# First adaptation of the second block on VectorE inside the first feed-forward, and output weight parts 0 and 1 split whole among the small products

## What is computed

```python
# first block, two layers
h = rms_norm(x, ln1_gain[l]); proj = h @ w_in[l]          # 1024 -> 2866
x = x + concat(nsa(proj), mla(proj), retention(proj)) @ w_out[l]
h = rms_norm(x, ln2_gain[l])
x = x + square(relu(h @ w_up[l])) @ w_down[l]              # 1024 -> 4096 -> 1024

# second block, layers ab and cd, on tokens x and context xc
shift, scale, gate = split(silu(c) @ w_ada + b_ada, 3)     # the adaptation: 1024 -> 3072
cshift, cscale, cgate = split(silu(c_ctx) @ w_ada + b_ada, 3)
h = rms_norm_2(x, norm_g) * (1 + scale) + shift            # hc likewise from xc
```

## Time and profile before

| | us |
|---|---|
| runs | 1077.96, 1077.51, 1077.50 |
| median | 1077.51 |
| span of the profiled execution | 1076.1 |
| its own time | not listed apart; the median lies 1.4 above the span |
| TensorE busy | 1051.7 (98%) |
| VectorE busy | 751.0 (70%) |
| ScalarE busy | 549.1 (51%) |

### The profile page before, as it was taken

The page is one execution under the profiler, slowest core; times in us unless marked ns, Lnnn a source line. Parts: engine busy times, 40 slices in busy tenths (PEclk is TensorE's granted clock), DMA queues, the critical chain, the costliest instruction groups (busy, mean ns, idle before and its releaser), DMA issues. The chain is left out here.

```text
span 1076.1 us, 17324 instructions
## 1 busy us (share of the span) xinstructions
PE 1051.7 (98%) x6788; PEld 900.5 (84%) x6788; DVE 751.0 (70%) x1442; ACT 549.1 (51%) x993; POOL 63.4 (6%) x80
## 2 busy tenths in 40 slices
PE   8999999999999999999999999999999999999996
PEld 7877889899988886888998899888886687989865
DVE  5766757655556576777788888789898945824765
ACT  5543845544445454764444544452657833623563
POOL 1000000000000000001000000020051301000000
PEclk9999999999999999999999999999999999999998
DMA  9758056565564657325856566593326233943200
GB/s 344 263 197 344 3 157 195 162 201 191 192 196 163 196 196 266 120 84 185 185 196 196 160 199 197 189 305 133 110 93 260 78 118 107 257 140 118 60 21 40
DMA packets 55477, 183.33 MB, mean 170 GB/s; under 512 B 21092, under 2 KB 33764, under 8 KB 35940
## 3 DMA queue, kind: packets, MB, share of 16 engines
q1 hardware_dynamic: 55396, 182.22, 51.8%
HBM read 179.31 MB, written 2.90 MB: 169 GB/s over the span
## 5 line engine op out<-in xcount | busy, mean ns | idle before, releaser
L257 DVE TENSOR_TENSOR w_lo<-ring,w_hi 128x1024 fp32r<-128x1024 f32 x259 | 316.2, 1223 | 179.8 <-ACT w_hi L242 176.2
L242 ACT CAST w_hi<-ring 128x1024 fp32r<-128x1024 f32 x259 | 270.9, 1054 | 318.0 <-PE banks L313 317.5
L313 PE MATMUL banks<-f_hi,w_hi 128*128 128x256 f32 x512 | 144.0, 281 | 0.0
L313 PE MATMUL banks<-f_hi,w_lo 128*128 128x256 f32 x512 | 143.8, 281 | 0.0
L313 PE MATMUL banks<-f_lo,w_hi 128*128 128x256 f32 x512 | 143.8, 281 | 0.0
L313 PE MATMUL banks<-w_hi,u_hi 128*128 128x512 f32 x256 | 100.1, 391 | 0.0
L313 PE MATMUL banks<-w_hi,u_lo 128*128 128x512 f32 x256 | 99.9, 390 | 0.0
L313 PE MATMUL banks<-w_lo,u_hi 128*128 128x512 f32 x256 | 99.9, 390 | 0.0
L313 PEld LDWEIGHTS banks<-f_hi,w_hi 128*128 128x128 f32 x512 | 96.4, 188 | 0.7 <-DVE f_lo L444 0.2
L313 PEld LDWEIGHTS banks<-f_lo,w_hi 128*128 128x128 f32 x512 | 96.5, 188 | 0.5
L313 PEld LDWEIGHTS banks<-f_hi,w_lo 128*128 128x128 f32 x512 | 96.5, 188 | 0.0
(11 more groups left out here) (421 smaller groups left out, 2167.9 us busy)
## 6 DMA issues: line engine op xcount, KB each, us to landing
ring<-in_w_up SPq DMA_DIRECT2D x32, 1024.0 KB, 5.2
ring<-in_w_down SPq DMA_DIRECT2D x32, 1024.0 KB, 5.1
ring<-in_w_in SPq DMA_DIRECT2D x23, 1024.0 KB, 5.2
ring<-in_ab_ada SPq DMA_DIRECT2D x12, 1024.0 KB, 5.9
ring<-in_cd_ada SPq DMA_DIRECT2D x12, 1024.0 KB, 5.2
ring<-in_cd_in SPq DMA_DIRECT2D x12, 1024.0 KB, 5.6
ring<-in_w_out SPq DMA_DIRECT2D x8, 1024.0 KB, 7.5
ring<-in_ab_in SPq DMA_DIRECT2D x16, 512.0 KB, 4.8
```

The costliest lines, as they stand in the source:

```text
L242: nc.scalar.copy(w_hi[:, n % PARTS, :], part_source(key, q)).then_inc(hi_ready, 1)
L257: nc.vector.tensor_tensor(w_lo[:, n % PARTS, :], part_source(key, q), w_hi[:, n % PARTS, :].bitcast(F32), ALU.subtract).then_inc(part_read ...
L313: mm = nc.tensor.matmul(dst, a, b, start=first_one and i == 0, stop=last_one and i == 2, skip_group_check=shares_bank)
```

## The change

- The adaptation leaves the mixers of both layers: the products, the copies, the turning, the bias additions, their signals and their places in the ring are gone. The attention loses the split in pieces.
- In the mixers ScalarE casts output part 0 behind its tanh and part 1 behind the first turned heads; VectorE makes the two low parts behind the retention's centred values, ahead of the activation of the hidden products. The first output half is handed back to the ring after the compressed values.
- In the first feed-forward the twelve halves of ab_ada stand in the ring, each behind the feed-forward half named by ADA_BEHIND (1, 3, 5, 8, 10, 13, 15, 17, 20, 22, 25, 27). VectorE multiplies eight row blocks of 128 x 512 for each slab and condition by a factor per partition and sums them in `ada_sums`: 96 instructions, two behind each of four consecutive parts around a half.
- TensorE sums over the partitions by 48 products with a column of -0.5: five slabs behind part 1 of the last down slab, the sixth after the last part, ahead of keep_busy. VectorE scales by -2 and adds the biases in one instruction at the stage's end.
- In both feed-forwards ScalarE takes the square, behind its own relu.

The diff, cut to its core:

```diff
-LAYER_SLABS = [("w_in", W_IN_SLABS), ("ada_turn", 1), ("cmp_k", 1), ("cmp_v", 1), ("small", 1), ("ada_small", 1),
-               ("ada_mix", 1), ("w_out", 2), ("ffn", 16)]
+LAYER_SLABS = [("w_in", W_IN_SLABS), ("cmp_k", 1), ("cmp_v", 1), ("small", 1), ("w_out", 2), ("ffn", 16)]
...
+ADA_SLABS = 3 * D // BANK
+ADA_BEHIND = [1 + m * 29 // (2 * ADA_SLABS) for m in range(2 * ADA_SLABS)]
...
+                if key == ("ffn", 0) and len(half_at[key]) - 1 in ADA_BEHIND:
+                    m = len(ada_at)
+                    ada_at.append(len(halves))
+                    halves.append((ADA_NAMES[0], m // 2, m % 2 * HALF, HALF))
...
+        def adapt_on_vector(dve, sums_of, done):
+            n = 0
+            for m, i in enumerate(ada_at):
+                for kk in range(KC // 2):
+                    k = m % 2 * (KC // 2) + kk
+                    w = ring[:, i % SLOTS, kk * BANK:(kk + 1) * BANK]
+                    if kk == 0:
+                        half_here(dve, i)
+                    for v in range(2):
+                        to, factor = sums_of[:, m // 2, v, :], cond[:, k, v:v + 1]
+                        if k == 0:
+                            last = nc.vector.tensor_scalar(to, w, factor, None, ALU.mult)
+                        else:
+                            dve.wait_ge(done, n - 1)
+                            last = nc.vector.scalar_tensor_tensor(out=to, in0=w, scalar=factor, in1=to, op0=ALU.mult,
+                                                                  op1=ALU.add)
+                        last.then_inc(done, 1)
+                        n += 1
+                        if kk == KC // 2 - 1 and v == 1:
+                            dve.wait_ge(done, n)
+                            dve.sem_inc(half_used, 1)
+                        yield
+
+        def ops_behind(half, part):
+            return 2 * sum((half, part) in ((b - 1, 1), (b, 0), (b, 1), (b + 1, 0)) for b in ADA_BEHIND)
+
+        def sum_conditions(pe, sums_of, s, to):
+            for f in range(4):
+                for v in range(2):
+                    n = 2 * (4 * s + f) + v
+                    mm = nc.tensor.matmul(to[:, n:n + 1], sums_of[:, s, v, f * P:(f + 1) * P], minus_half[:, 0:1],
+                                          start=True, stop=True)
+            return mm
...
-                    adapt_products(pe, ada_key, 0, 7)
...
-                    pe.wait_ge(kept, 1)
-                    turn_conditions(adapted(0), banks[:, 7, :]).then_inc(turned, 1)
...
-                    pe.wait_ge(ada_ready, 1)
-                    adapt_products(pe, ("ada_small", layer), 0, 7, signal=False)
...
-                    dve.wait_ge(turned, 1)
-                    add_biases(0, 3 * layer, banks[:, 7, 0:16]).then_inc(ada_ready, 1)
+                    for q in range(AHEAD):
+                        split_lo(dve, ("w_out", layer), q, signal=False)
                     if layer:
-                        dve.wait_ge(ada_ready, 1)
                         find_scales(0)
...
+                    dve.wait_ge(half_used, h_small + 1)
+                    half_split(dve, ("w_out", layer), AHEAD - 1)
                     retain_vector(dve)
...
-                    keep_adapted(act, ada_key, 0, 7, adapted(0)).then_inc(kept, 1)
+                    split_hi(act, ("w_out", layer), 0)
...
                     copy_heads(1)
+                    split_hi(act, ("w_out", layer), 1)
...
-                adapt_products(pe, ada_key, 0, ADA)
...
-                turn_conditions(adapted(1), banks[:, ADA_TURNED, 0:16])
                 turn_heads(2)
-                turn_conditions(adapted(2), banks[:, ADA_TURNED, 16:32]).then_inc(mix_turned, 1)
...
+                            if not beside and i == 2 * FFN_GROUPS - 1 and q == 1:
+                                pe.wait_ge(relu_ready, FFN_GROUPS)
+                                pe.wait_ge(adapted, 16 * (ADA_SLABS - 1))
+                                for s in range(ADA_SLABS - 1):
+                                    sum_conditions(pe, ada_sums, s, ada_columns)
...
-                        keep_busy(0, 4)
+                        pe.wait_ge(adapted, 16 * ADA_SLABS)
+                        sum_conditions(pe, ada_sums, ADA_SLABS - 1, ada_columns).then_inc(columns_ready, 1)
+                        keep_busy(1, 4)
...
+                        act.wait_ge(relu_ready, g + 1)
+                        if g >= 1:
+                            act.wait_ge(u_ready, g)
+                        nc.scalar.activation(square[:], relu[:], ACT.Square).then_inc(square_ready, 1)
...
-                        dve.wait_ge(relu_ready, g + 1)
-                        nc.vector.tensor_tensor(square[:], relu[:], relu[:], ALU.mult).then_inc(square_ready, 1)
...
                             advance(taps, 2)
+                            advance(adaptation, ops_behind(2 * i + q // 2, q % 2))
...
                         advance(taps, 2)
+                        advance(adaptation, ops_behind(2 * i + 1, 1))
...
+                    if not beside:
+                        dve.wait_ge(columns_ready, 1)
+                        nc.vector.scalar_tensor_tensor(
+                            out=ada[:, 0, :, :], in0=ada_columns.rearrange("p (f v) -> p f v", v=2), scalar=-2.0,
+                            in1=feats2[:, 0:4 * ADA_SLABS].unsqueeze(2).broadcast_to([P, 4 * ADA_SLABS, 2]), op0=ALU.mult,
+                            op1=ALU.add)
```

More of the change, by code:

```diff
@@ L101, in slab_plan @@
 def slab_plan():
-    halves, first, first_part, n_parts = [], {}, {}, 0
+    halves, first, first_part, half_at, ada_at, n_parts = [], {}, {}, {}, [], 0
     uses = [((name, layer), name, layer * n, n) for layer in range(DEPTH) for name, n in LAYER_SLABS]
@@ L120, in slab_plan @@
             for c0 in (0, HALF):
+                half_at.setdefault(key, []).append(len(halves))
                 if name == "ffn":
@@ L127, in slab_plan @@
                     halves.append((name, at + (W_IN_AT[i] if name == "w_in" else i), c0, HALF))
[L128 removed]
+                if key == ("ffn", 0) and len(half_at[key]) - 1 in ADA_BEHIND:
+                    m = len(ada_at)
+                    ada_at.append(len(halves))
+                    halves.append((ADA_NAMES[0], m // 2, m % 2 * HALF, HALF))
+    return halves, first, first_part, half_at, ada_at
 def build_program(nc, dram, out):
[L132 removed]
+    plan, first, first_part, half_at, ada_at = slab_plan()
     with ExitStack() as ctx:
@@ L209, in load_first_part, with load_behind @@
             sp.dma_start(ring[:, 0, cols], dram[name][at, :, cols]).then_inc(first_parts_here[q], 16)
-        def load_behind(sp, key, n_slabs, halves=2):
-            for i in range(first[key], first[key] + halves * n_slabs):
+        def load_behind(sp, key, n_slabs, between=0):
+            for i in range(first[key], first[key] + 2 * n_slabs + between):
                 load_half(sp, i + SLOTS)
@@ L223, in part_source @@
         def part_source(key, q):
-            return ring[:, (first[key] + q // 2) % SLOTS, (q % 2) * PART:(q % 2 + 1) * PART]
+            return ring[:, half_at[key][q // 2] % SLOTS, (q % 2) * PART:(q % 2 + 1) * PART]
         def split_hi(act, key, q):
@@ L237, in split_hi @@
             elif q % 2 == 0:
-                half_here(act, first[key] + q // 2)
+                half_here(act, half_at[key][q // 2])
             if n >= PARTS:
@@ L1829, in mixers @@
                             causal, plain_weigh(NSA_H * HD + h * HD, (0, 1))))
[L1830 to L1842, removed]
                     def attention(signals, banks_here):
-                        return attend(signals, units, (probs, probsT, nmax, total, inverse), next_low, next_high, banks_here)
+                        return attend(signals, units, (probs, probsT, nmax, total, inverse), banks_here)
                     def retain(signals, here):
@@ L2201, in _ @@
                 def _(sp):
-                    for i in range(first["ada_turn", layer], first["ada_mix", layer]):
+                    for i in range(first["cmp_k", layer], first["w_out", layer]):
                         load_half(sp, i + SLOTS)
@@ L2388, in _ @@
                     copy_heads(5)
-                    keep_adapted(act, ("ada_small", layer), 0, 7, adapted(1)).then_inc(row_kept, 1)
                     retain_scalar(act)
@@ L2420, in compress_and_retain @@
             kept_sums = sums[:, 40:40 + NR]
-            ADA, ADA_TURNED = 6, 5
-            ada_key = ("ada_mix", layer)
             def faded_of(h):
@@ L2799, in _ @@
                         ctx_gate(1)
+                    adaptation = iter(()) if beside else adapt_on_vector(dve, ada_sums, adapted)
                     for i in range(2 * FFN_GROUPS):
```

84 lines of the change are left out of this document (25 added, 59 removed).

## The result

The changed kernel takes 1091.23 us (median of four runs, 1089.68 to 1093.42) against 1077.51: a ratio of 1.0127, with a 95% interval of 1.0112 to 1.0141. Forecast were 1083.4 us and a range that ended at 1089: slower, as forecast, but by 13.7 us instead of 5.9.

What follows compares the result with a forecast made beforehand. TensorE was taken to bound the kernel. Mixers -6.3, sums +9.7 and VectorE +2.5 make +5.9 us, taking the span from 1076.1 to 1082.0; 1.4 more gives a median of 1083.4 us, range 1077 to 1089.

Steps and rivals of the forecast that it cites:

- the price of the sums: End of the first feed-forward: 48 products on TensorE at 0.101 us a record add 9.7 us, 8.1 for forty.
- The ends, a twentieth either way: Bounds on the sums' cost in the first feed-forward: 9.2 and 10.2 us.
- The mixers: Small products and retention, up to the attention: TensorE gets back 3.3 us in layer 0, 3.0 in layer 1, 6.3 together.
- a sign of error: Behind the mixers' new waits: a granted clock below 1.00 would show the forecast wrong; no size given.
- before the compressed products: Mixers: TensorE waits 1.5 us for VectorE's activation chain, which first does two whole output splits.
- VectorE in the feed-forward: First feed-forward: 96 added products at 0.67 us each make TensorE wait, mostly early; 2.5 us, ends 0.3 to 14.
- The transfers: First feed-forward: 12 MB more raise the DMA share from 0.59 to some 0.81; nothing added to the time.
- The second feed-forward: It loses its squares on VectorE; nothing gained, as TensorE is paced by its own products.
- From span to median: Whole kernel: the median lies 1.4 us above the profiled span, 1083.4 from 1082.0.
- Rival 1: First feed-forward: VectorE or the ring becomes its bound; 1087 to 1095 us at 0.80 to 0.90 a product; chance 0.12.
- Rival 2: First feed-forward's sums: columns are cheap at 0.030 us a record, 2.9 us in all; 1076.6 us, no change; chance 0.10.
- Rival 3: Mixers and feed-forward: forecast waits are covered, 12.7 us back against 9.7 paid; 1074.5 us, faster; chance 0.07.

Runs made afterwards that it cites:

- six_blocks: The change with mixer waits filled by keep-busy products, VectorE's adaptation products later without pauses, and sums in six blocks of eight; 1081.41 us.
- spread_sums: The change with its 48 sums placed one at a time between dense products of the first feed-forward's last three slabs; 1086.30 us.
- spread_late: spread_sums with VectorE's twelve windows of adaptation products starting at the seventh weight half and following without a pause; 1084.88 us.
- one_sum: The change with 47 of the 48 sums left out and VectorE's products kept; 1074.29 us.
- block_filled: six_blocks with the sums where the change has them, 40 behind part 61 and eight behind the last part; 1088.48 us.

## Why the prediction was right or wrong

**The step that failed is the price of the sums**: "Forty of them (8.1 us) stand between parts 61 and 62 of a stage in which TensorE never waits, so they are added whole", with ends of 9.2 and 10.2 us for all 48. The record was priced rightly, as 0.106 us in six_blocks at a granted clock of 1.00 shows. But the row it came from has eight such records between other work, and its clock was carried over to 80 in a row. In the change the block takes 12.88 us, the dense products behind it lose 2.2, and the whole costs 17.0 us instead of 9.7. The ends, a twentieth either way, bounded the record and not the clock.

**The mixers** were right in mechanism and sizes. At a clock of 1.00 layer 0 gives back 3.2 us (29.00 in spread_sums) and layer 1 3.1 (29.12 in the change), against 3.3 and 3.0. The change itself gets only 2.2 in layer 0, because the clock fell behind the new waits. The prediction named that as a sign of error and gave it no price and no chance. One wait was mis-sized: before the compressed products it was 0.63 and 0.76 us where the prediction put 1.5, with 0.40 and 0.17 more behind them.

**VectorE in the feed-forward**: 2.5 us forecast, 2.4 measured in two ways (spread_sums less spread_late, one_sum less before). The sum fits better than its terms: the waits are 0.58 us for part 3 (0.7 forecast) and 1.02 in the third slab (1.5), the 0.3 us at the first activation has no wait of its own in the trace, and 0.8 us of the 2.4 stand in no wait. **The transfers** cost nothing, as forecast: no wait of TensorE or VectorE in the stage ends with one. **The second feed-forward**, where nothing was forecast, gave 0.7 us (211.72 to 211.03 between the transposes that open it and the next stage); neither trace has a wait inside it that accounts for this, and the cause stays open. **From span to median** the sum adds 1.4 us, where the change's profiled execution lies 1.8 above its span: 0.4 us of the miss.

The account of the profiled span: -2.2 and -3.1 in the mixers, +17.0 for the sums, +2.4 for VectorE and -0.7 in the second feed-forward make +13.4; measured is +13.1, and the rest lies in small shifts elsewhere.

**The rivals.** Rival 1 would have given a time in the measured range, but nothing of its mechanism is there: 0.665 us a product, and no wait for low halves behind the third slab. Rival 2 fell with 0.106 us a record. The 25 ns of the Trainium skill, TensorE: Matmul & The Clock Gate, section Back-to-back issue gap, are not reached here, where each product is fp32 and has a fresh stationary side of 128 columns; the section itself says that its figures for isolated products leave out the load of that side. Rival 3 fell with the waits. What was missing is a rival on the clock. The same page of the Trainium skill, section Why this matters for your kernels, warns of idle gaps between bursts of matmuls. Neither fall would follow from that row: the mixers' longest wait, 2.03 us, is shorter than the gaps it names, and in the block the windows show no gap.

## What to carry to other kernels

A row of tiny products counts as busy time in a profile and can still let the granted clock fall, and then the dense products behind it run at half speed too: spread such products (singly or in blocks of 16 records here), or turn the operands around so that the long side moves. Before work is taken from TensorE where it would otherwise wait, ask what will keep its clock up: fourteen filler products a layer, idle ones put into the waits, brought the executions from 5.6 to 0.9 us apart. A price read off a row holds at that row's clock, so the clock of the new place is a term of its own, with its own ends.

## What was not expected of the hardware

- The granted clock fell from 1.00 to 0.50 while TensorE counted as busy without a break, in the change and again in block_filled, while six blocks of the same products left it at 1.00.
- In the mixers, whose program is the same in the change, spread_sums, one_sum and spread_late, it fell in one layer or the other, in the one profiled execution of each, at a cost of 1.0 us (layer 0, 30.01 less 29.00) to 1.35 us (layer 1, 30.47 less 29.12); with the other waits filled it fell behind the one that was left.
- Twelve fp32 products with 32 stationary and 512 moving columns do the sums of 48 products with one moving column: 24 records cost 2.8 us (1.85 for 16 and 1.0 for 8), where the 48 products cost 10.9 at a clock of 1.00 (192.74, less 184.25 and plus the 2.4 of VectorE's start). Their results still have to be turned, for 0.33 us more in layer 1's mixers.
